# Pads between SBUF tiles: the gemm operands of a two-block transformer kernel at other distances modulo 512 bytes

## The reference, cut to what matters

```python
# first block
u = rmsnorm(h, norm_mix)
u_ssm, q, k, v = jnp.split(u @ w_in, ...)
y_ssm, y_attn = s5_branch(u_ssm, ...), stick_breaking_attention(q, k, v)
gates = jax.nn.sigmoid(u @ w_gate + b_gate)
h = h + (g_ssm * (y_ssm @ w_up_ssm) + g_attn * (y_attn @ w_up_attn)) @ w_out
hid = jax.nn.relu(rmsnorm(h, norm_mlp) @ w_ff1)
h = h + (hid * hid) @ w_ff2
...
# second block: a gated linear attention layer, then a forgetting attention layer
h = h + gla_mixer(rms_norm(h, g0), ...)
h = h + (p[0] @ ple_proj[0]) * jax.nn.sigmoid(rms_norm(h, ple_norm[0]) @ ple_gate[0])
h = h + fox_mixer(rms_norm(h, g1), ...)
h = h + (p[1] @ ple_proj[1]) * jax.nn.sigmoid(rms_norm(h, ple_norm[1]) @ ple_gate[1])
return rms_norm(h, final_norm)
```

## Time and profile before

| | |
|---|---|
| median of the runs | 1419.55 us (1418.07 to 1422.56) |
| span of the profiled execution | 1417.8 us (no other time of that execution is given) |
| TensorE matmuls, busy | 1382.5 us, 98%, 7012 of them |
| TensorE weight loads, busy | 1166.7 us, 82% |
| VectorE busy | 958.5 us, 68% |
| ScalarE busy | 739.6 us, 52% |
| GpSimd busy | 65.9 us, 5% |
| data moved | 118.38 MB, 83 GB/s |
| mean granted TensorE clock | 0.995 |

### The profile page before, as it was taken

How to read it: one execution, slowest core, us unless ns; L and a number is a source line. 1 busy time by engine, 2 the same in 40 slices (tenths; PEclk the granted TensorE clock), 3 DMA queues, 4 the chain that set the end, 5 groups by cost and what they waited for, 6 DMA issues and landing times.

```text
span 1417.8 us, 18409 instructions
## 1 busy us (share of the span) xinstructions
PE 1382.5 (98%) x7012; PEld 1166.7 (82%) x7012; DVE 958.5 (68%) x1329; ACT 739.6 (52%) x1050; POOL 65.9 (5%) x77
## 2 busy tenths in 40 slices
PE   7999999999999999999999999999999999999997
PEld 4888888888888888888888889888878888887876
DVE  7989984424553544444467777564879999999574
ACT  6777776232333223222255434343558888888353
POOL 2000000000200000000000100012100000000311
PEclk9999999999999999999999999999999999999998
DMA  6111102222322232223221211222221121211311
GB/s 230 41 60 60 60 16 104 89 90 94 114 89 90 89 119 89 89 89 110 98 90 60 90 60 60 104 89 89 90 89 60 63 85 59 80 68 35 129 60 60
DMA packets 19307, 118.38 MB, mean 83 GB/s; under 512 B 2400, under 2 KB 3680, under 8 KB 5680
## 3 DMA queue, kind: packets, MB, share of 16 engines
q1 hardware_dynamic: 18960, 116.51, 23.2%
q0 software_dynamic: 288, 1.05, 0.2%
HBM read 115.45 MB, written 2.10 MB: 83 GB/s over the span
## 4 chain that ended last, share of the span: by engine, by line
PE 76%; DVE 8%; ACT 3%; issue 1%; DVEq 0%; POOL 0%; ACTq 0%
PE ps L531 23%; PE ps L533 23%; PE ps L532 23%; DVE wlo L1945 1%; PE ps L1071 1%; PE ps L1104 1%; PE ps L1061 1%; PE ps L1102 1%; PE ps L1063 1%; PE ps L613 0%; ACT uhi L1241 0%; DVE st L2463 0%; ACT sthi L1241 0%; ACT whi L1241 0%; DVE stlo L2466 0%
## 5 line engine op out<-in xcount | busy, mean ns | idle before, releaser
L531 PE MATMUL ps<-uhi,whi 128*128 128x512 f32 x1060 | 421.8, 398 | 4.7 <-DVE ulo L2507 1.6
L533 PE MATMUL ps<-uhi,wlo 128*128 128x512 f32 x1060 | 414.5, 391 | 0.0
L532 PE MATMUL ps<-ulo,whi 128*128 128x512 f32 x1060 | 413.8, 390 | 0.0
L1945 DVE TENSOR_TENSOR wlo<-wraw,whi 128x2048 fp32r<-128x2048 f32 x104 | 242.0, 2329 | 99.2 <-ACT whi L1241 97.8
L1241 ACT ACTIVATE whi<-wraw 128x2048 fp32r<-128x2048 f32 x105 | 200.5, 1909 | 165.5 <-PE ps L533 163.6
L531 PEld LDWEIGHTS ps<-uhi,whi 128*128 128x128 f32 x1060 | 199.6, 188 | 49.0 <-DVE wlo L1945 3.1
L533 PEld LDWEIGHTS ps<-uhi,wlo 128*128 128x128 f32 x1060 | 199.5, 188 | 43.0
L532 PEld LDWEIGHTS ps<-ulo,whi 128*128 128x128 f32 x1060 | 200.0, 189 | 38.5
L531 PE MATMUL ps<-hdhi,whi 128*128 128x512 f32 x256 | 99.6, 389 | 0.0
L533 PE MATMUL ps<-hdhi,wlo 128*128 128x512 f32 x256 | 99.6, 389 | 0.0
L532 PE MATMUL ps<-hdlo,whi 128*128 128x512 f32 x256 | 99.6, 389 | 0.0
(11 more groups left out here) (485 smaller groups left out, 2529.9 us busy)
## 6 DMA issues: line engine op xcount, KB each, us to landing
wraw<-wstream SPq DMA_DIRECT2D x105, 1024.0 KB, 4.8
h<-xT SPq DMA_DIRECT2D x4, 512.0 KB, 5.4
outT<-h SPq DMA_DIRECT2D x8, 256.0 KB, 2.9
s5b<-s5p_d SPq DMA_DIRECT2D x1, 1024.0 KB, 11.9
pe_in<-pT POOLq DMA_DIRECT2D x2, 512.0 KB, 3.8
cst_in<-cst_d SPq DMA_DIRECT2D x5, 64.0 KB, 10.1
reset<-cst_d SPq DMA_DIRECT2D x1, 256.0 KB, 11.2
wa<-wa_d SPq DMA_DIRECT2D x1, 160.0 KB, 6.0
```

Of the source, the lines that this page charges most:

```text
L531: nc.tensor.matmul(out, lh, rh, start=start, stop=False, skip_group_check=True)
L532: nc.tensor.matmul(out, lh, rl_, start=False, stop=False, skip_group_check=True)
L533: mm = nc.tensor.matmul(out, ll, rh, start=False, stop=stop, skip_group_check=True)
L1945: V.tensor_tensor(wlo[:, slot, :], wraw[:, slot, :], whi[:, slot, :], ALU.subtract).then_inc(lo_done, 1)
```

## The change

Six pads are put between tiles and pad1 is taken out. The whole diff:

```diff
         h = sb("h", [P, DC, T])
+        sb("pad_uhi", [P, 8])
         uhi = sb("uhi", [P, DC, T], F32R)
+        sb("pad_ulo", [P, 8])
         ulo = sb("ulo", [P, DC, T], F32R)
         wraw = sb("wraw", [P, 2, UW])
+        sb("pad_whi", [P, 16])
         whi = sb("whi", [P, 2, UW], F32R)
+        sb("pad_wlo", [P, 32])
         wlo = sb("wlo", [P, 2, UW], F32R)
@@
         s5r = sb("s5r", [P, 2, S5_PAIRS], F32R)
-        sb("pad1", [P, 48])
@@
                 mg = glu
+                sb("pad_mhi", [P, 100], F32, s)
                 mhi = sb("mhi", [P, DC, T], F32R, s)
                 mlo = sb("mlo", [P, DC, T], F32R, s)
@@
             hd = sb("hd", [P, 2, T], F32, s)
+            sb("pad_hdhi", [P, 16], F32, s)
             hdhi = sb("hdhi", [P, 4, T], F32R, s)
+            sb("pad_hdlo", [P, 64], F32, s)
             hdlo = sb("hdlo", [P, 4, T], F32R, s)
```

## The result

The changed kernel takes 1432.35 us, the median of four runs (1432.01 to 1432.65); the kernel before took 1418.99 beside it (1418.07 to 1422.56). The ratio is 1.0086, with a 95% interval of 1.0070 to 1.0103: 13.4 us slower. The forecast was 1419.5, no change, with a range from 1412 to 1430. The change made the kernel slower, and the time lies above the range.

The account below looks back on a forecast made before the run. The prediction took TensorE, busy 98%, to bound the kernel through its gemm matmuls. All terms were nothing, so the 1417.8 us span changed by 0 and the time was 1419.5, range 1412 to 1430.

Parts of the forecast that it names:

- What bounds the kernel: Whole span: TensorE busy 98%, so altered gemm matmul spacing moves the end nearly one for one; VectorE and ScalarE have slack.
- The gemm's matmuls: Lines 531 to 533, 4788 matmuls of 512 columns and 384 of 256: spacing unchanged at 0.2267 and 0.1200 us, cost nothing.
- the four rows: Trace evidence on whether operand distance sets the gemm's surplus of some 13 ns: three for a constant, none for a dependence.
- the bounds: For the gemm's matmuls: nothing, a gain of 11.7 ns each (the surplus over 0.215), or a loss, nearest row 6 ns.
- the faster rival: Gemm stream and weight load collide at distance 0; other distances free 11.7 ns each, 57.5 us, so 1362; chance 0.10.
- The busy stretch: 1068 to 1276 us, VectorE busy 93%, ScalarE 84%: gaps still 0.2267, taken as evidence against collisions in memory.
- The surplus is the same for 256 and 512 columns: Gemm matmuls carry some 13 ns over their columns at either width, read as looking like a fixed cost per matmul.
- VectorE, ScalarE, the weight DMA, the clock: Outside the gemm: engines between -1 and +1%, DMA hidden by some 6 us, clock not moved on purpose; cost nothing.
- slower, distance 0 is the good one: Gemm stream and weight load may meet at other distances: 6 ns on 4532 matmuls, 27 us, so 1447; chance 0.11.
- 0.23 or more wherever the distance is not 0: Start-to-start time in us of gemm matmuls that would show the slower case, with 0.2267 again after hdhi with whi.
- the change does less than it says: Gemm pairs: if collisions go by a unit other than 32 bytes, few pairs change; 1419.5 too, inside the 0.79.

Follow-up runs that it names:

- The finer bench: Matmuls only, kernel's computation left out: distances in steps of 4 bytes, 64 triples, float32, narrower weights; the wide triple takes 680.0 to 706.8 ns.
- the bench: Matmuls only, other engines idle: fixed operand distances and the changed kernel's triples; u takes 686.6 ns, hd 693.4, all at distance 0 680.0.
- the worst layout: Kernel before with uhi at 192, ulo and wlo at 128 bytes modulo 256 from whi, scoped tiles at 0: 1444.00 us against 1419.92, ratio 1.0165.

## Why the prediction was wrong

**What bounds the kernel: right, and it made the miss linear.** Any change of the gemm's spacing was to move the end nearly one for one; the gaps summed to 13.2 us, the span moved by 13.1.

**The gemm's matmuls: this step failed.** The term that it put at nothing was the effect of the distance between a float32r stream and its weights. It said "I take nothing, since of the four rows three speak for a constant and none for a dependence". The measured term is +14.8 us for the 512-column matmuls and -0.7 for those of 256 columns. The four rows, in turn:
- *Lines 672 and 697* are float32. The finer bench shows float32 to be blind to the distance (0.4292 us at all five, with 512 columns), so they could say nothing of float32r.
- *Line 587* is float32 as well. "Distance 0 costs float32 nothing" held, and it held at the four other distances tried as well. The step "half of that, 0.215, is one pass" was wrong besides: function unread issues 8 matmuls and the trace has 16 records of line 587, so the 0.43 is one of the two records of a matmul. No row shows a 512-column pass of 0.215, and the gain of 11.7 ns that the bounds and the faster rival took from it has no row behind it.
- *The busy stretch* tested other engines' traffic. The effect is there with TensorE's own stream and weight load alone; the bench has it in full with all other engines idle.
- *The surplus is the same for 256 and 512 columns.* At distance 0 it is. At others it isn't: at 192 bytes 256 columns take 113.4 ns, half of their surplus gone, and 512 columns 233.4. An equality at one distance can't show that a cost is fixed.

What the trace held was that no float32r matmul stood at another distance. From that followed an unknown with bounds on both sides, and not a chance of 0.79 for its middle.

The rule of the Trainium skill (SBUF — State Buffer, "Who interferes with whom") that TensorE's two read ports never wait on anyone gave nothing, too. The measurement decides: with no other engine at work the same triple takes from 680.0 to 706.8 ns as its distances change in steps of 64 bytes.

**VectorE, ScalarE, the weight DMA, the clock: right.** 2330, 1913 and 689 ns and 4.8 us against 2329, 1909, 689 and 4.8; the mean granted clock is 0.994 against 0.995.

**The rival "slower, distance 0 is the good one": right in kind and place, twice too dear.** It took 6 ns for each of 4532 matmuls, 27 us. hd came out as it said and more (13.4 ns a triple in the bench, 13.6 in the kernel, of which the hdhi and whi pair paid 0.6). But 3180 of the matmuls are those of u, and their distances of 160, 192 and 32 modulo 256 make a mild triple: 6.6 ns in the bench and in the kernel, 7.0 us in place of 19. Its sign "0.23 or more wherever the distance is not 0" failed for ulo with whi, which stayed at 226. It came true for hdlo with whi, but not for its reason: that pair is at 256, as good as 0, and rose to 233 beside a neighbour at 384. Its chance, 0.11, rested on the same misused rows.

**The rival "faster, a collision removed": wrong for 512 columns.** No single distance in steps of 4 bytes is below the 226.6 of distance 0. For 256 columns something of it is true, and it was worth 1.0 us, not 4.5.

**The rival "the change does less than it says": half right.** The period is 256 bytes and not 512, so hdlo with whi didn't move. But there is no unit of 32 bytes under which distances are alike: 28 and 32 bytes differ by 20 ns a triple in the bench.

**What stays open.** What the mechanism is (which accesses of stream and load meet, and where) isn't shown, only its period, that the difference of addresses counts and not the place, and that it is float32r's alone of the two types tried. Nor is it shown what picks one of several steady rhythms at one distance. The surplus of 13 ns over the columns that stays at distance 0 went away with no distance and with no smaller load. And a stretch of chopped gemms pays less than the bench's sum; that short matmuls and waits there are the reason is argued, not tested.

## What to carry to other kernels

Where a kernel is a stream of float32r matmuls, each with a weight load of its own, start the moving and the stationary tiles at the same place modulo 256 bytes, and guard that when small tiles are added: one tile moved by 32 bytes cost 0.8% here. Judge spacing from start to start, not by durations, and take a price only from rows of the same number type. Three benches of nothing but matmuls took 2.1 ms of chip time and gave the map. Sum it by triples as they stand in the kernel, since values of single pairs (233 to 234 ns for each of u's) would have tripled the term. Take the sum for a guide and not for the price: it was right for the 512-column matmuls of the change (14.9 against 14.8 us), and too high for the worst layout (34.7 against 24.1).

## What the runs showed of the hardware

- A 512-column float32r matmul with its own weight load takes 226.7 ns at best at 2.4 GHz, and 226.6 to 240.0 as the distance modulo 256 bytes of its two operands changes; the map has no order at steps of 4 bytes (28: 226.6, 32: 233.4, 64: 228.6, 132: 240.0).
- One distance can have more than one steady rhythm: 108 bytes settled at 226.7 in one bench and 233.3 in another, and the u triple with uhi 32 bytes off at 700 and at 688 ns within one kernel.
- A pair at a bad distance can also lengthen the gap before it: +4.6 ns for line 532 when only its neighbours' uhi had moved by 32 bytes.
- Best distances depend on the column count: 0, among others, for 512 columns, while 256 columns fall from 119.7 to 113.4 at 192 (weights 64 bytes further than the stream).
- Float32 with 512 columns takes 0.4292 us a record at 0, 32, 64, 128 and 192 bytes.
- The size of the weight load, 128 down to 32 columns, doesn't shorten a 512-column float32r matmul (226.7 against 229.7 to 231.8).
